# Retention's output products regrouped: values first, then states, with the two heads alternating

## What is computed

```python
scores = einsum('bnihd,bnjhd->bnhij', qc, kc) * intra_decay
intra = einsum('bnhij,bnjhe->bnihe', scores, vc)
k_w = exp((C - 1.0 - idx)[:, None] * log_g[None, :])
u = einsum('bnjhd,bnjhe->nbhde', kc * k_w[:, :, None], vc)
# s_before: state ahead of each chunk, s <- chunk_decay * s + u
q_w = exp((idx + 1.0)[:, None] * log_g[None, :])
cross = einsum('bnihd,nbhde->bnihe', qc * q_w[:, :, None], s_before)
out = (intra + cross).reshape(B, L, H, -1)
```

## Time and profile before

| | |
|---|---|
| runs of the kernel | 3484.59, 3488.89, 3490.75 us |
| median | 3488.89 us |
| span of the profiled execution | 3485.7 us |
| TensorE matmuls busy | 3306.7 us (95%) |
| TensorE weight loads busy | 2962.1 us (85%) |
| VectorE busy | 1735.5 us (50%) |
| ScalarE busy | 950.5 us (27%) |
| GpSimd busy | 877.8 us (25%) |
| mean granted TensorE clock | 0.978 |

### The profile page before, as it was taken

How to read it: one execution, slowest core, us unless ns; L and a number is a source line. 1 busy time by engine, 2 the same in 40 slices (tenths; PEclk the granted TensorE clock), 3 DMA queues, 4 the chain that set the end, 5 groups by cost and what they waited for, 6 DMA issues and landing times.

```text
span 3485.7 us, 50000 instructions
## 1 busy us (share of the span) xinstructions
PE 3306.7 (95%) x19286; PEld 2962.1 (85%) x19286; DVE 1735.5 (50%) x3073; ACT 950.5 (27%) x1698; POOL 877.8 (25%) x478
## 2 busy tenths in 40 slices
PE   6999988799999999999999999989999999999998
PEld 3978887566879999999988788976678999999997
DVE  4735256565467555555583452236545733333335
ACT  3132111465352111111131410137634311111112
POOL 1311313122222223232222123222213222323221
PEclk8999999899999999999999999999999999999999
DMA  5511558633311222222222114672341111111111
GB/s 203 178 34 40 198 172 270 185 72 73 69 49 67 85 78 79 83 72 84 73 74 68 34 54 137 189 212 55 73 92 32 36 43 43 45 45 42 48 43 68
DMA packets 135684, 313.64 MB, mean 90 GB/s; under 512 B 52716, under 2 KB 73524, under 8 KB 132448
## 3 DMA queue, kind: packets, MB, share of 16 engines
q1 hardware_dynamic: 90848, 224.38, 21.9%
q10 hardware_dynamic: 44672, 87.03, 7.7%
HBM read 240.24 MB, written 57.90 MB: 86 GB/s over the span
## 4 chain that ended last, share of the span: by engine, by line
PE 82%; DVE 8%; ACTq 3%; DMA 3%; ACT 2%; issue 1%; SPq 1%; POOL 0%; DVEq 0%; POOLq 0%; PEldq 0%
PE ps L1355 19%; PE ps L1330 19%; PE ps L1271 9%; PE ps L994 6%; PE ps L1050 4%; PE ps L1248 3%; PE ps L1141 3%; PE ps L1204 3%; PE ps L1184 3%; PE ps L1306 2%; PE ps L976 2%; PE ps L1018 1%; DMA crossed<-straight 1%; DVE act_lo L2368 1%; PE ps L924 1%
## 5 line engine op out<-in xcount | busy, mean ns | idle before, releaser
L747 POOL CAST w_hi<-raw 128x1024 fp32r<-128x1024 f32 x212 | 231.2, 1090 | 2109.2 <-PEq L1361 489.3
L2183 DVE SCALAR_TENSOR_TENSOR x<-ps,mod,x 128x352 f32<-128x352 f32 (+2 forms) x768 | 353.5, 488 | 427.3 <-PE ps L1355 345.9
L750 POOL TENSOR_TENSOR w_lo<-raw,w_hi 128x1024 fp32r<-128x1024 f32 x212 | 528.8, 2495 | 36.7 <-POOL w_hi L747 36.7
L1355 PE MATMUL ps<-act_hi,w_hi 128*128 128x352 f32 x1536 | 500.9, 326 | 8.4 <-DVE act_lo L2368 8.4
L1355 PE MATMUL ps<-act_lo,w_hi 128*128 128x352 f32 x1536 | 497.9, 324 | 0.0
L1355 PE MATMUL ps<-act_hi,w_lo 128*128 128x352 f32 x1536 | 495.4, 323 | 0.0
L1330 PE MATMUL ps<-h_hi,w_hi 128*128 128x352 f32 x1344 | 434.8, 323 | 10.1 <-DVE x L2183 7.7
L1330 PE MATMUL ps<-h_lo,w_hi 128*128 128x352 f32 x1344 | 431.0, 321 | 0.0
L1330 PE MATMUL ps<-h_hi,w_lo 128*128 128x352 f32 x1344 | 431.0, 321 | 0.0
L1821 ACT ACTIVATE relu_b<-ps,consts 128x352 f32<-128x352 f32 x192 | 106.5, 555 | 1140.3 <-PE ps L1330 1120.8
L1271 PE MATMUL ps<-pT,vb 128*128 128x512 f32 (+5 forms) x1080 | 399.0, 459 | 8.5 <-ACT pT L1735 8.5
(11 more groups left out here) (220 smaller groups left out, 6078.0 us busy)
## 6 DMA issues: line engine op xcount, KB each, us to landing
raw<-in_w SPq DMA_DIRECT2D x212, 512.0 KB, 3.7
ada_next<-in_w_ada SPq DMA_DIRECT2D x48, 512.0 KB, 4.3
ada_w<-in_w_ada SPq DMA_DIRECT2D x24, 512.0 KB, 5.8
kb<-scr_k SPq DMA_DIRECT2D x36, 328.0 KB
kb<-scr_k SPq DMA_DIRECT2D x60, 164.0 KB
qb<-scr_q SPq DMA_DIRECT2D x36, 264.0 KB
ada_nat<-in_w_ada_first SPq DMA_DIRECT2D x8, 1024.0 KB, 20.6
qb<-scr_q SPq DMA_DIRECT2D x60, 132.0 KB
```

The costliest lines, as they stand in the source:

```text
L747: pool.tensor_copy(hi, raw[:, uc % 2, 0:width]).then_inc(pool_hi, 1)
L750: pool.tensor_tensor(lo, raw[:, uc % 2, 0:width], hi.bitcast(F32), ALU.subtract).then_inc(w_ready, 1)
L1355: last = mm(ps[:, i % 6, 0:GW], w[:, k * 256 + o * 128:k * 256 + o * 128 + 128], (act_lo if low else act_hi)[:, k * T + g * GW:k * T + (g ...
L2183: last = v.scalar_tensor_tensor(xs, ps[:, bank, a - g * GW:b - g * GW], gs, xs, ALU.mult, ALU.add)
```

## The change

In `outputs`, the loops are reordered. Before, for each tile and head the product with values was followed by the (one or two) products with states of the same tile and head. After, all products with values of the batch are issued (tiles outside, heads inside), and then all products with states (tiles, then chunks, then heads). The number and the shapes of the products are the same. Since the products of a batch now share a bank while unfinished, the start flag is set only for the first tile of the batch.

```diff
@@ -918,8 +918,12 @@
                             hs = slice(64 * h, 64 * h + 64)
                             p0 = 256 * h + 128 * (t % 2) if t < 8 else TS * h
                             mm(ps[hs, O_BANK[i], c0:c0 + r], v_all[0:r, t, 128 * j + 64 * h:128 * j + 64 * h + 64],
-                               p_dec[0:r, b % 2, p0:p0 + r], start=True, stop=False, skip_group_check=True)
-                            for cp in range(2 if t < 8 else 1):
+                               p_dec[0:r, b % 2, p0:p0 + r], start=(t == BATCHES[b][0]), stop=False, skip_group_check=True)
+                    for t in BATCHES[b]:
+                        for cp in range(2 if t < 8 else 1):
+                            for h in range(2):
+                                c0 = 128 * (t % 4)
+                                hs = slice(64 * h, 64 * h + 64)
                                 w = 64 if t < 8 else TS
                                 last = mm(ps[hs, O_BANK[i], c0 + 64 * cp:c0 + 64 * cp + w],
                                           states[hs, 2 * t + cp if t < 8 else 17, :],
```

## The result

The changed kernel takes 3441.9 us (median of 4 runs, 3440.4 to 3442.5) against 3488.3 for the kernel before (4 runs, 3484.6 to 3490.8): a ratio of 0.9872, 95% interval 0.9858 to 0.9886. The profiled execution spans 3440.1 us, where the prediction had 3439.8; the time that it forecast was 3443.

A forecast was written before the change was run, and what follows sets the result against it. TensorE was taken to bound both retention stretches. 24 full batches (42.2 us), 6 small ones (2.7) and 1.0 for the low clock sum to 45.9: span 3485.7 to 3439.8, plus 3.2 gives 3443; own range 3436 to 3450, wider 3436 to 3458.

The forecast's parts named there:

- The bound: Both retention stretches: TensorE is the limit, busy 171.4 of 176 us and 165.4 of 170.
- (a): Full batch of outputs: six fewer shape changes at 0.15 us each, 0.90 us saved per batch.
- (b): Full batch of outputs: the two heads overlap, saving 0.44 us in the values and 0.44 us in the states.
- the two numbers: TensorE blocks: 0.15 us per shape change, plus 0.055 us per step with 64 moving columns or 0.11 with 128.
- The unknown of (b): Values' step on both column halves: taken as 0.11 us, bounded by 0.055 and 0.16; bounds of -5 and +5 us.
- (c): One-tile batch of outputs: four blocks of 0.23 us become two, 0.45 us less each, 2.7 us over 6.
- The low-clock batch: One of 24 full batches, 4.55 us at the lower clock: saves 2.7 us rather than 1.76, 1.0 more.
- The rule on program order: Outputs blocks: strict order of matmuls would cost 4 us over 24 batches, 3447 not 3443; chance 0.08 together with slow instruction supply.
- Issue-bound: Outputs batches: TensorE's sequencer supplies short records too slowly, 1.49 us per batch, 3450 in all; chance 0.08 together with program order.
- The clock: Retention stretches: shorter outputs bring the granted clock down more often, up to 3608 us with all 300 us low; chance 0.04.

The follow-up runs named there:

- head by head: Changed kernel with four blocks per batch: values then states of head 0, then the same of head 1, never two heads in one block; 3467.3 us, ratio 0.9954.
- tile by tile: Changed kernel with separate values and states blocks for each tile, heads alternating, so four blocks per full batch; 3445.1 us, ratio 0.9884.
- heads in turn: Changed kernel with heads not alternating: in each block all products of head 0, then all of head 1; 3447.2 us, ratio 0.9895.
- states first: Changed kernel with the states products ahead of the values products in each batch; 3435.5 us, ratio 0.9858.
- runs of two: Kernel with all of one head before the other, but its states block alternates two products of each head; 3439.7 us, ratio 0.9868.
- the kernel with one block: Changed kernel with states before values and the updates moved up to them, all 64x64 products of a gap in one block; 3430.0 us, ratio 0.9846.

## Why the prediction was right

*The bound.* TensorE was the bound of both stretches: 46.0 us taken out of its work there came out of the kernel as 45.6 us of span, with the same waits as before.

*(a) and (b), the two numbers.* 0.15 us per change of shape and a step of 0.055 or 0.11 us gave 1.18 us for a batch; it is 1.20, since the states' step is 0.0575. The split was tested by taking each part alone. Without overlap (head by head) the batch is 2.37 us, with two more changes of shape (tile by tile) 1.50. From 2.94, fewer changes of shape bring 0.57 us with two of the six still missing, the overlap of heads then 0.87 (2.37 to 1.50), and the last two changes 0.30. So six changes are 0.87 us and the overlap 0.87: half and half, where the prediction had 0.90 and 0.88.

The 0.15 us is a fixed part read off these blocks; that it is the filling and draining of the array, as the prediction called it, no run separates.

*The unknown of (b).* The values' step on both column halves, bounded by 0.055 and 0.16, was 0.11: the block of four steps is 0.59 us.

*(c)* 0.47 us for the one-tile batch, 0.46 predicted.

*The low-clock batch.* The prediction let the batch at the lower clock keep that clock. It ran at full clock in the changed kernel, saving 3.35 us (4.55 to 1.20) rather than 2.7. The projection item behind it, which had run at the lower clock too (5.3 us instead of 4.1), stands in no term of the prediction. One fall less was worth about 3 us (25 us gained in layer 0, 22 in layer 1); the prediction's bound for a fall was 2.5. So the two stretches gained 47.0 us; the stages between them gave 1.3 more, those behind layer 1's took back 2.5, and 45.6 came out at the end. That the span is within 0.3 us of 3439.8 is luck. The time was 3441.9 and not 3443 because the 3.2 us that the prediction added to the span lay between a median and one execution; the profiled run of the changed kernel took 1.8 us more than its span.

*The rule on program order.* The Trainium skill, "TensorE: Matmul & The Clock Gate", section on packing small matmuls, has matmuls start and end strictly in program order. The prediction took L898's 0.66 us over it, and the kernel with heads in turn confirms that: its values' block (0.60 us, 0.92 by the rule) shows no loss. The kernel with states first shows it record by record, with a states record ahead of six updates issued before it. But the reading was right only up to a length: with four products in a row on one half, 5 of the 8 steps that could overlap are lost. Alternating heads was therefore not needed for the values, and for the states it saved 0.28 us per batch against whole heads in turn, but only 0.05 against runs of two.

*Issue-bound.* Refuted for blocks of this length: 24 records came within 1.20 us, and 16 within 0.61, 0.04 us each, under the 0.06 of the earlier trace rows; in the kernel with one block a whole gap of 50 records takes 2.62 us, 0.052 each. Whether a queue filled during the item helps was not tried. The prediction's price took 0.062 us where its rows give (0.69 - 0.20) / 8 = 0.061, which changes it by 0.4 us. The 62 ns that it set beside this, from the Trainium skill, "TensorE: Matmul & The Clock Gate", section "Wait — 56ns, not 53.3ns?", stand there for hardware decode off only; no run here shows which decode was on.

*The clock.* It did not turn against the change: falls in the two stretches were one instead of two. The low stretch behind layer 0's, at 321 us, is a new one, which the prediction did not look for; the stage that it lies in was 0.3 us longer. What triggers a fall stays open; it came behind idle times of 1.6 and 2.3 us in some executions and not in others.

## What to carry to other kernels

Count blocks of equal array shape, not matmuls: each change of shape costs 0.15 us here, as much as two and a half of the small products' steps, and products of one shape from different parts of the code (updates and outputs) can share a block. Within a block put products for different halves of the array next to each other, or at most two of one half in a row. A timeline read from start to start, fitted with one fixed cost and a step per shape, gave 45.9 us where the batches shrank by 46.0, and that this would come out as time was known from the waits of the stretch, which had been looked at first.

## What the runs showed of the hardware that was not expected

Work on one half of the array is held back by a long run on the other: two fp32 products of one head (four records) cost the other head nothing (0.60 us for the block), runs of two in a longer block cost one step (0.66 instead of 0.61), a run of four cost five (0.89), and head 1 began with head 0's fifth record. That each half holds four records of its own fits all three, and is not shown beyond them. Products that share no part of the array do not even start in the order in which they were issued (states ahead of updates, 27 ns behind the first of them).

Halving the moving columns of a 64x64 product changed its step by nothing (16 weight loads in 0.54 us either way), and two records in one step take no longer than one. What sets the step is open: the loading of 64 weight columns or a fixed least time of a half. No run changes the weights alone, and turns with 128 weight columns came 0.06 us apart.
